# Norms of a two-layer diffusion trunk: root and shift applied behind the matmuls, weight splits and attention reordered

## What is computed

```python
h = rms_norm(x, norm1_g[l]) * (1.0 + sc1) + sh1
out = mixer(h)                       # layer 0: HGRN2 + mLSTM; layer 1: windowed attention + MLA
x = x + g1 * out
h = rms_norm(x, norm2_g[l]) * (1.0 + sc2) + sh2
x = x + g2 * (silu(h @ w1) * (h @ w3)) @ w2      # ffn, inner width 2816
```

## Time and profile before

| what | value |
|---|---|
| median of three runs | 1130.74 us (1130.0 to 1131.2) |
| profiled execution | 1131.77 us, of which the profile's span is 1130.0 us |
| mean granted clock of TensorE | 0.982 of full speed |
| TensorE matmuls (PE) | 1065.7 us busy, 94% of the span, 6725 instructions |
| weight loads (PEld) | 974.1 us, 86% |
| GpSimd (POOL) | 539.6 us, 48% |
| VectorE (DVE) | 421.9 us, 37% |
| ScalarE (ACT) | 396.5 us, 35% |
| chain that ended last | PE 83%, DVE 6%, ACT 3%, DMA 3%, POOL 2% |

### The profile page before, as it was taken

The page is one execution under the profiler, slowest core; times in us unless marked ns, Lnnn a source line. Parts: engine busy times, 40 slices in busy tenths (PEclk is TensorE's granted clock), DMA queues, the critical chain, the costliest instruction groups (busy, mean ns, idle before and its releaser), DMA issues.

```text
span 1130.0 us, 16311 instructions
## 1 busy us (share of the span) xinstructions
PE 1065.7 (94%) x6725; PEld 974.1 (86%) x6725; DVE 421.9 (37%) x850; ACT 396.5 (35%) x630; POOL 539.6 (48%) x422
## 2 busy tenths in 40 slices
PE   4799999997989999999999899799989999999997
PEld 3598899876979999999999799655879999999997
DVE  3757898148661111111112433177571111111122
ACT  0531333356343332332213451477333333332121
POOL 0364538541545555555557242203254566565662
PEclk9899999999999999999999999989989999999999
DMA  8633454456656666655666732502042454534441
GB/s 309 229 115 116 148 171 152 142 186 230 200 150 186 187 186 188 188 186 164 203 209 188 194 113 60 142 1 75 15 135 75 121 141 112 141 98 128 122 128 56
DMA packets 202053, 166.40 MB, mean 147 GB/s; under 512 B 20269, under 2 KB 184188, under 8 KB 201852
## 3 DMA queue, kind: packets, MB, share of 16 engines
q1 hardware_dynamic: 189568, 136.79, 40.6%
q10 hardware_dynamic: 12412, 28.58, 7.4%
HBM read 162.43 MB, written 2.92 MB: 146 GB/s over the span
## 4 chain that ended last, share of the span: by engine, by line
PE 83%; DVE 6%; ACT 3%; DMA 3%; POOL 2%; issue 1%; ACTq 0%; SPq 0%; DVEq 0%
PE banks L456 22%; PE banks L458 21%; PE banks L457 21%; PE banks L550 3%; PE banks L527 2%; PE banks L529 2%; PE banks L528 2%; POOL w_lo L1134 2%; PE banks L694 2%; DMA raw<-in_ada_w 2%; DVE ht L1651 1%; DVE h_lo L1642 1%; PE banks L543 1%; DMA xtok<-in_x_sample 1%; PE banks L995 1%
## 5 line engine op out<-in xcount | busy, mean ns | idle before, releaser
L1134 POOL TENSOR_TENSOR w_lo<-raw,w_hi 128x512 fp32r<-128x512 f32 (+2 forms) x398 | 514.2, 1323 | 574.3 <-ACT w_hi L1158 574.3
L456 PE MATMUL banks<-h_hi,w_hi 128*128 128x384 f32 (+1 forms) x1040 | 353.3, 340 | 6.2 <-DVE h_lo L1642 3.5
L458 PE MATMUL banks<-h_hi,w_lo 128*128 128x384 f32 (+1 forms) x1040 | 348.4, 335 | 0.0
L457 PE MATMUL banks<-h_lo,w_hi 128*128 128x384 f32 (+1 forms) x1040 | 348.3, 335 | 0.0
L1158 ACT ACTIVATE w_hi<-raw 128x2048 fp32r<-128x2048 f32 (+3 forms) x112 | 188.1, 1679 | 249.0 <-PE banks L458 135.8
L456 PEld LDWEIGHTS banks<-h_hi,w_hi 128*128 128x128 f32 (+1 forms) x1040 | 195.0, 188 | 17.2 <-issue 14.3
L457 PEld LDWEIGHTS banks<-h_lo,w_hi 128*128 128x128 f32 (+1 forms) x1040 | 195.0, 188 | 1.0
L458 PEld LDWEIGHTS banks<-h_hi,w_lo 128*128 128x128 f32 (+1 forms) x1040 | 194.9, 187 | 0.6
L1705 DVE TENSOR_TENSOR uf<-sa,banks 128x384 f32<-128x384 f32 x44 | 24.4, 554 | 325.3 <-PE banks L458 318.9
L456 PE MATMUL banks<-u_hi,w_hi 128*128 128x384 f32 x352 | 119.4, 339 | 0.0
L458 PE MATMUL banks<-u_hi,w_lo 128*128 128x384 f32 x352 | 118.2, 336 | 0.0
(11 more groups left out here) (328 smaller groups left out, 1192.9 us busy)
## 6 DMA issues: line engine op xcount, KB each, us to landing
raw<-in_ffn_w SPq DMA_DIRECT2D x88, 512.0 KB, 5.1
raw<-in_ada_w SPq DMA_DIRECT2D x28, 1024.0 KB, 6.2
raw<-in_ffn_w SPq DMA_DIRECT2D x32, 704.0 KB, 4.6
vada_raw<-in_ada_w ACTq DMA_DIRECT2D x20, 1024.0 KB, 6.7
raw<-in_w_in_even SPq DMA_DIRECT2D x18, 1024.0 KB, 5.2
raw<-in_w_out_even SPq DMA_DIRECT2D x4, 1024.0 KB, 6.2
raw<-in_w_in_odd SPq DMA_DIRECT2D x3, 1024.0 KB, 5.5
raw<-in_w_in_odd SPq DMA_DIRECT2D x8, 256.0 KB, 5.9
```

The costliest lines, as they stand in the source:

```text
L456: pe.matmul(out, s_hi, m_hi, start=first and j == 0, stop=False)
L457: pe.matmul(out, s_hi, m_lo, start=False, stop=False)
L458: mm = pe.matmul(out, s_lo, m_hi, start=False, stop=last and j == len(terms) - 1)
L1134: ins = pool.tensor_tensor(low_part(s)[:, at:to], raw[u % RAW][:, at:to], high(s)[:, at:to].bitcast(F32), ALU.subtract)
```

## The change

It does these things:

- Norms 1, 2 and 3 no longer make `h`. Behind each residual ScalarE makes `xg_hi`, the rounded `X` times gain, and DVE `xg_lo`, the rest (`gained`, `gained_low`). Two columns behind the 384 tokens hold the high and low part of the two shift vectors, so a normed feature is a product of 386 columns (`TS`); its last two columns are the shift's product with the weight.
- The reciprocal root is made in `rs` (with two ones behind it). DVE multiplies each finished bank by it (`scale`, and the two scalings in `ffn`); the shift's product is then added per context and latent columns: by ScalarE as the bias of silu or of the take, by DVE in the product of gate and up.
- `stat` moves between the fourth and fifth k of the first pair.
- ScalarE's split of the second `up` unit moves behind the eighth high part; the splits before it stand between the high parts.
- In `in1` the value projection becomes a feature like the others; its result is transposed (`vc_turned`). TensorE, ScalarE and DVE wait on `taken` where they waited for a bank to be read.
- In attention TensorE issues the values of job n-3 before the transposes of job n-2, and ScalarE rounds a finished tile's high part at the start of its step.
- `u_hi` and `u_lo` of the first eight inner tiles lie in `h_hi` and `h_lo`; some buffers are laid out anew.

```diff
+TS, TX = T + 2, 400
...
+IN1_TAKES = [("cq", 0), ("cq", 1), ("cq", 2), ("ckv", 0), ("ckv", 1), ("kr",),
+             ("qc", 0), ("qc", 1), ("qc", 2), ("qc", 3), ("kc",), ("vc",)]
...
+        rs = flat(ht)[:, 0:TS]
...
+            def normed_features(keys, u, ready, n):
+
+                first_features(keys, u, ready, 0, 4, (xg_hi, xg_lo), TS)
+                stat(n)
+                first_features(keys, u, ready, 4, DT, (xg_hi, xg_lo), TS)
+
+            def normed(key, u, c):
+                features(key, u, c, x=(xg_hi, xg_lo), n=TS)
...
             def ffn(l, ready):
-                first_features([("gate", l, 0), ("up", l, 0)], number[(f"up{l}", 0)], ready)
+                normed_features([("gate", l, 0), ("up", l, 0)], number[(f"up{l}", 0)], ready, 2 * l + 1)
                 for f in range(1, FT):
                     u = number[(f"up{l}", f)]
-                    features(("gate", l, f), u, 0)
-                    features(("up", l, f), u, P)
+                    normed(("gate", l, f), u, 0)
+                    normed(("up", l, f), u, P)
...
-            modulation("norm1", between=lambda: stat(1))
+            modulation("norm1")
...
-            bk = None
-            for c in range(NCH):
-                bk = tokens(("vc",), in1(2), P, P, c, out=None if c == 0 else (bk, P * c), last=c == 2)
-            dense.was_read(pe, ("qc", 3))
+            normed(("vc",), in1(2), P)
+            was_taken(("qc", 3))
+            was_taken(("kc",))
+            was_taken(("vc",))
+            turn(misc, ("vc_turned",), [(c * P, vcT[:, c * P:(c + 1) * P]) for c in range(NCH)])
...
                 if n < len(jobs):
                     scores(n, jobs[n])
+                if n >= VALUE_LAG:
+                    values(n - VALUE_LAG, jobs[n - VALUE_LAG])
                 if 0 <= n - TURN_LAG < len(jobs):
                     turned(n - TURN_LAG, jobs[n - TURN_LAG])
-                if n >= VALUE_LAG:
-                    values(n - VALUE_LAG, jobs[n - VALUE_LAG])
...
-            stat(3)
...
+            def gained(key, n, m):
+
+                dense.was_read(act, key)
+                for c, a, b in ((1, 0, TC), (0, TC, T)):
+                    ins = act.activation(xg_hi[:, m, a:b], X[:, m, a:b], ACT.Copy, scale=gain[:, n, m, c:c + 1])
+                ins.then_inc(S["hhi_ready"], 1)

             def out_projection(l, n):
+                split_to(split_index[number[(f"out{l}", 2)]] + 1)
+                gained(("out", l, 0), n, 0)
+                gained(("out", l, 1), n, 1)
+                split_to(split_index[number[(f"up{l}", 0)]] + 1)
+                gained(("out", l, 2), n, 2)
+                split_to(split_index[number[(f"out{l}", 3)]] + 1)
+                gained(("out", l, 3), n, 3)
+                for m in range(4, DT):
+                    gained(("out", l, m), n, m)
                 split_to(split_index[number[(f"up{l}", 1)]] + 1)
+                root(n, rs[:, 0:T])
...
-                    bk = dense.filled(act, ("gate", l, f))
-                    if f >= 2:
-                        dense.was_read(act, ("up", l, f - 2))
-                    act.activation(sa[:, f % 2, :], bk[:, 0:T], ACT.Silu).then_inc(dense.read(("gate", l, f)), 1)
-                    dense.was_read(act, ("up", l, f))
-                    act.activation(u_hi[:, f, :], uf[:, f % 2, :], ACT.Copy).then_inc(S["uhi_ready"], 1)
+                    i = f % 2
+                    dense.was_read(act, ("gate", l, f))
+                    for c, a, b in ((1, 0, TC), (0, TC, T)):
+                        ins = act.activation(sa[:, i, a:b], sa[:, i, a:b], ACT.Silu, bias=sa[:, i, T + c:T + c + 1])
+                    ins.then_inc(S["silu_ready"], 1)
+                    act.wait_ge(S["uf_ready"], FT * l + f + 1)
+                    act.activation(u_hi(f), uf[:, i, 0:T], ACT.Copy).then_inc(S["uhi_ready"], 1)
...
+                    if l == 0:
+                        if m < DT - 1:
+                            split_to(split_index[number[("down0", 2 * m + 3)]] + 1)
+                        gained(("down", 0, m), 2, m)
...
-            def take(key, dst):
-                evacuate(dense, key, dst, lambda b: b[:, 0:T])
+            def take(key, dst, p=0):
+                i = IN1_TAKES.index(key) % 2
+                dense.was_read(act, key)
+                for c, a, b in ((1, 0, TC), (0, TC, T)):
+                    ins = act.activation(dst[:, a:b], xt[p:, i, a:b], ACT.Identity, bias=xt[p:, i, T + c:T + c + 1])
+                ins.then_inc(S["taken"], 1)
...
+                m = n - VALUE_LAG
+                if m >= 0 and ends[m][1]:
+                    bk = pvs.filled(act, ("pv", job_tile[m]))
+                    act.activation(mix_part(h_hi, job_tile[m]), mix_bank(bk, job_tile[m]), ACT.Copy)\
+                        .then_inc(S["pv_hi"], 1)
...
+            def gained_low(n, m):
+
+                if m == 0:
+                    shift_columns(n)
+                dve.wait_ge(S["hhi_ready"], 8 + 8 * n + m + 1)
+                for c, a, b in ((1, 0, TC), (0, TC, T)):
+                    ins = dve.scalar_tensor_tensor(xg_lo[:, m, a:b], X[:, m, a:b], gain[:, n, m, c:c + 1],
+                                                   xg_hi[:, m, a:b].bitcast(F32), ALU.mult, ALU.subtract)
+                ins.then_inc(S["h_ready"], 1)
...
+                dve.wait_ge(S["rstd_ready"], 2 * l + 2)
                 for f in range(FT):
-                    dense.was_read(dve, ("gate", l, f))
-                    bk = dense.filled(dve, ("up", l, f))
-                    if f >= 2:
-                        dve.wait_ge(S["u_ready"], FT * l + f - 1)
-                    dve.tensor_tensor(uf[:, f % 2, :], sa[:, f % 2, :], bk[:, 0:T], ALU.mult)\
-                        .then_inc(dense.read(("up", l, f)), 1)
+                    i = f % 2
+                    bk = dense.filled(dve, ("gate", l, f))
+                    dve.tensor_tensor(sa[:, i, 0:TS], bk[:, 0:TS], rs, ALU.mult).then_inc(dense.read(("gate", l, f)), 1)
                     if f:
                         low_u(f - 1)
+                    bk = dense.filled(dve, ("up", l, f))
+                    dve.tensor_tensor(uf[:, i, 0:TS], bk[:, 0:TS], rs, ALU.mult).then_inc(dense.read(("up", l, f)), 1)
+                    dense.was_read(dve, ("up", l, f))
+                    dve.wait_ge(S["silu_ready"], FT * l + f + 1)
+                    for c, a, b in ((1, 0, TC), (0, TC, T)):
+                        ins = dve.scalar_tensor_tensor(uf[:, i, a:b], uf[:, i, a:b], uf[:, i, T + c:T + c + 1],
+                                                       sa[:, i, a:b], ALU.add, ALU.mult)
+                    ins.then_inc(S["uf_ready"], 1)
...
+            def scale(key, p=0):
+                i = IN1_TAKES.index(key)
+                bk = dense.filled(dve, key)
+                if i >= 2:
+                    dve.wait_ge(S["taken"], i - 1)
+                dve.tensor_tensor(xt[p:, i % 2, 0:TS], bk[p:, 0:TS], rs[p:], ALU.mult).then_inc(dense.read(key), 1)
...
+            dve.wait_ge(S["rstd_ready"], 3)
+            for key in IN1_TAKES[0:5]:
+                scale(key)
+            scale(("kr",), 96)
+            low_rank(0, 0, 3)
+            scale(("qc", 0))
+            low_rank(1, 3, 5)
...
+            scale(("qc", 1))
+            scale(("qc", 2))
             dve.wait_ge(S["odd_in"], 16)
-            for i in range(5):
+            rope(0)
+            scale(("qc", 3))
+            rope(1)
+            scale(("kc",))
+            rope(2)
+            scale(("vc",))
+            for i in range(3, 6):
                 rope(i)
-            rope(5)
             modulation("cq")
```

More of the change, by code:

```diff
@@ L479, in features, with first_features @@
                 release[u] = (dense.done, dense.at[key] + 1)
-            def first_features(keys, u, ready, first=0, end=DT):
+            def first_features(keys, u, ready, first=0, end=DT, x=(h_hi, h_lo), n=T):
                 if first == 0:
-                    first_outs[:] = [dense.fill(pe, key)[:, 0:T] for key in keys]
+                    first_outs[:] = [dense.fill(pe, key)[:, 0:n] for key in keys]
                 for k in range(first, end):
@@ L859, in _, with was_taken @@
             out_projection(0)
-            modulation("norm1", between=lambda: stat(1))
+            modulation("norm1")
             ffn(0, 16)
-            modulation("norm2", between=lambda: stat(2))
+            modulation("norm2")
             in1 = lambda i: number[("in1", i)]
             turn_s, turn_m = cst("swa_turn"), cst("mla_turn")
+            def was_taken(key):
+                pe.wait_ge(S["taken"], IN1_TAKES.index(key) + 1)
             def rotate(key, matrix, src):
@@ L1192, in out_projection, with first_norm @@
-            def out_projection(l, n):
+                act.activation(out, out, ACT.Exp, scale=-0.5).then_inc(S["rstd_ready"], 1)
+            def first_norm():
+                root(0, rstd[:, 0, :])
+                for m in range(DT):
```

(22 more changed lines are left out.)

128 lines of the change are left out of this document (60 added, 68 removed).

## The result

The changed kernel took 1124.73 us in the median of five runs (1123.68 to 1125.14) against 1130.24 of the kernel before beside it (1128.24 to 1131.2): a ratio of 0.9949, interval 0.9927 to 0.9971. That is 5.5 us faster where 16.1 were forecast. The profiled execution took 1123.68, span 1121.9.

A forecast was written before the change was run, and what follows sets the result against it. TensorE was taken as the bound, busy nearly the whole span, with time to win only at idle stretches. 4.7 + 4.7 + 5.9 + 2.6 + 1.3 - 2.1 - 1.0 = 16.1 us off the median 1130.74 gave 1114.7, range 1109 to 1123.

The forecast's parts named there:

- Rival (a): Norm's work only moves: DVE falls behind among POOL's pieces, late raw buffer holds the third unit; 1122.5 us, chance 0.22.
- The loops: Normed matmuls: two more columns on 2400 matmuls cost 0.87 ns each by the slope, 2.1 us in all.
- Wrong if a 386-column matmul comes every 0.18 us or more: Sign against the forecast in the normed loops; 0.174 us per 386-column matmul was expected.
- rival (b): All 2400 normed matmuls: 386 columns cost a step, 13.8 ns each, 33 us; 1146 us, chance 0.07.
- Seams 1 and 3: From each output projection to its feed-forward: the first pair no longer waits for statistics; gains 4.7 and 5.9 us.
- if a gate feature waits for a bank: Sign against the forecast at the feed-forwards' gate features; the three banks were expected to be read by DVE within a feature.
- Seam 2: From the last down projection to `in1`: 15.3 us after the change, a hole of about 2.1 for `ada_row`; gain 4.7.
- The moved splits: Feed-forward's `up` units: second unit's split moves later, third lands at about 334; cover 1.2 us, so no cost taken.
- `in1`: Value projection as one feature takes 4.2 us instead of 8.1; less 1.3 for what hangs on it, gain 2.6.
- wall of `uq`: Behind `in1`: the second `uq` is fetched when the first ada buffer is released, so its wait moves along.
- Attention: Values fill TensorE's waits for `pr`, DVE's waits for high parts go; net gain 1.3 us (ends -1 and +4).
- The rows at the end: At attention's end turn, copy and values stand in a row twice, costing 0.85 to 1.7 us more.

The follow-up runs named there:

- experiment 7: The changed kernel with the weight split of up's second unit two high parts earlier in both output projections: 1124.82 us, ratio 0.9954.

## Why the prediction was wrong

The forecast of 1114.7 (1109 to 1123) missed the measured 1124.73. Rival (a) with its 1122.5 is nearer in number, but not in mechanism: the seams gave what was forecast, and of (a) only the late raw unit came, for 1.0, and attention's missing gain. Step by step:

- **The loops: the step that failed.** "I take the slope, as 129 against 128 is nearest in kind": 0.87 ns on 2400 matmuls, 2.1 us. Measured 3.0 to 3.9 ns by stage, 8.6 us; removing two thirds of the extra columns gave 7 to 8 back. On rows 400 apart the slope for width was nearly right: 386 columns cost 0.9 to 1.7 more than 384, where it says 0.87. Not seen was that the operand's rows also move, from 384 to 400 columns apart (`TX = 400`), and that this counts. The Trainium skill ("TensorE: Matmul & The Clock Gate", section Wait — 56ns, not 53.3ns?) gives the distance of warm matmuls as columns over 2.4 GHz and about 2.5 ns. An estimate from that rule is 162.5 for 384 and 0.8 more for 386. Here both numbers are higher, 173.3 and 3.8 more, for fp32r. The forecast's test ("Wrong if a 386-column matmul comes every 0.18 us or more") was too coarse: 177 ns passes it and costs 9 us. Its rival (b) had the place right and a price of 13.8 ns; it would have turned the sign at 7.6.
- **Seams 1 and 3** were right in size. Seam 1: 12.6 forecast, 11.7 measured; the 0.7 for late ada weights didn't come, and `stat` costs 1.3 and not 1.5 (the pair with it takes 9.8, 48 steps of 0.177 and 1.3). Seam 3: gain 5.9, measured 6.8, but not by the wait that the forecast had: it charged 1.6 for `stat` waiting for the last square, and `stat` waited for nothing. DVE's pace among POOL's pieces was as forecast ("4.0 to 6 us a feature"), 4.8 to 5.9, and 2.63 behind them:
```profile
810.11 1.54 DVE L1727 TENSOR_TENSOR sq<-sq 128x384 f32<-128x384 f32 x1
811.68 1.80 DVE L1717 SCALAR_TENSOR_TENSOR xg_lo<-X,gain,xg_hi 128x128 fp32r<-128x128 f32 x2
...
828.12 0.56 DVE L1727 TENSOR_TENSOR sq<-sq 128x384 f32<-128x384 f32 x1
828.71 0.75 DVE L1717 SCALAR_TENSOR_TENSOR xg_lo<-X,gain,xg_hi 128x128 fp32r<-128x128 f32 x2
```
  The last square ended at 833.33, 1.2 ahead of `stat`, and TensorE paid 0.86 in front of the pair instead, most likely for a bank (it starts 0.1 behind DVE's last read of one). So "if a gate feature waits for a bank" came true in this small form. The rule of the Trainium skill that the prediction named for this ("SBUF — State Buffer", Who interferes with whom) is borne out again: 0.56 becomes 1.54 while POOL splits.
- **Seam 2**: 15.3 forecast, 16.7 in this profile, 15.0 to 15.1 in the five where the strips ran at full clock. The hole was forecast as 2.1 and is 1.94.
- **The moved splits**: "I take nothing; the cover is 1.2 us, and without it lateness is paid one for one". The raw unit was split at 332.94 (the forecast's 334 less the 1.4 by which this profile is earlier), and POOL began at 334.93; TensorE still lost 1.0 in feed-forward 0 (experiment 7). The first piece was there in time; the later ones were not, since TensorE takes a piece in about 1.06 us and POOL needs 1.3.
- **`in1`**: the term (2.6) was nearly right (2.2). Behind the strips the forecast had 0, and this profile has 2.1: 1.5 is a slow clock in the last part, 1.3 lies up to the end of the wait for `uq`, and the part between is 0.7 shorter. That the wall of `uq` "moves along" was right; neither the slow clock nor the long DMA issue in it was foreseen.
- **Attention**: 1.3 forecast, 0.3 to 0.4 measured for the order, and 0.8 lost ahead of it at the long output issue. The rows at the end ("0.85 to 1.7 more") and waits of the values took back more of the 3.3 us than thought.

With the columns at their price the forecast is 1114.7 + 6.5 = 1121.2, inside the range. The whole miss is 10.0 us. Two of these are no work: the forecast took 1.0 off because the kernel before's profiled execution lay 1.0 above its median, and the changed kernel's lay 1.05 below. The other 8.0 are the table's. Too little was forecast for the columns (6.5), the strips to attention (2.1), attention (1.4), seam 2 (1.3) and the late unit (1.0); too much for the start (1.9) and for seams 1 and 3 (0.9 each). That makes 8.6; the 0.6 over is not resolved, and some columns, those of the first pairs, are in it twice.

## What to carry to other kernels

When an operand gets wider, ask where its rows now lie, not only how many columns are added: a few ns on every matmul of a TensorE-bound loop outweighs a seam. Then measure the pair of width and distance in that loop, and don't go by a rule: putting the extra columns into one product of three cut their price from 3.8 to 0.6 ns at rows 400 apart, and the same pattern was the dearest, 4.0 over the kernel before, at 416 and 384. Before two profiles are compared stage by stage, compare the granted clock of the stage: here it hid a gain of 0.9 and feigned another of 1.0. And price an extra per matmul by its sum over the loop: a test that can't see 3 ns can't see 7 us.

## What was not expected of the hardware

- Matmuls of the same 384 fp32r columns come every 173.3 ns with rows 384 columns apart and every 176.0 with rows 400 apart, in a pattern of 12 that repeats (48 at 386 apart, none at 384). One product of 386 and two of 384 on the same 400 come at 173.9; with 416 and 384 apart at 177.3.
- One DMA issue of the second `uq` fetch took 1.2 to 1.8 us instead of 0.51 in ten of thirteen profiles of kernels with the change, and an output's issue on ScalarE's queue at attention's start 1.2 to 2.0 instead of 0.45 in eleven; in neither place in the one profile of the kernel before. What brings it about was not tried.
- The same 1.94 us hole in seam 2 was followed by slow strips (granted clock of 0.50 to 0.61 over 3 us) in five of ten profiles and by strips at full clock in the other five. Likewise the second output projection began at 0.74 or 0.75 over 6 us in three of thirteen profiles, and the last part before attention ran at 0.79 in three.
